# Three chunks of a chunked recurrence: decays laid out by token, their cumulative sums by TensorE with triangular maps

## What is computed

```python
w_log = -jax.nn.softplus(-(w0[:, None, None, :] + jnp.einsum('blde,def->dblf', jnp.tanh(w_in), w2))) - 0.5
decay = jnp.exp(-jnp.exp(w_log.astype(jnp.float32)))
...
sa = jnp.einsum('bhij,bhj->bhi', S, a_t)
S = S * w_t[:, :, None, :] + sa[..., None] * b_t[:, :, None, :] + v_t[..., None] * k_t[:, :, None, :]
```

## Time and profile before

| | us |
|---|---|
| median of 3 runs (lowest to highest) | 1172.7 (1168.99 to 1172.95) |
| the profiled execution | 1167.96 |
| its span, first to last instruction | 1166.2 |
| PE busy | 1102.9 (95%) |
| DVE busy | 644.8 (55%) |
| ACT busy | 336.8 (29%) |

### The profile page before, as it was taken

One profiled execution on the slowest core, in us unless ns is written; L12 is line 12 of the kernel. 1 busy time (PEld: TensorE's weight loads), 2 busy tenths in 40 slices (PEclk: granted clock), 3 DMA queues, 4 the chain that ended last, 5 costly groups with the idle time before them and its releaser, 6 DMA issues.

```text
span 1166.2 us, 15684 instructions
## 1 busy us (share of the span) xinstructions
PE 1102.9 (95%) x6231; PEld 759.6 (65%) x6231; DVE 644.8 (55%) x1358; ACT 336.8 (29%) x786; POOL 110.8 (9%) x107
## 2 busy tenths in 40 slices
PE   4899999989877989999999999999999999999998
PEld 2444858767866675465588888445465488888543
DVE  3222315688989876997146566702897136655400
ACT  2212213776643425243112211103434111122100
POOL 0000100220120020450000000100450000000000
PEclk9899999999889999999999999999999999999999
DMA  9822342000004223633265543326423344554310
GB/s 355 288 73 73 131 144 77 2 1 1 3 1 122 90 74 144 217 107 110 73 197 187 162 150 144 145 72 216 145 73 119 103 139 158 163 170 159 144 36 37
DMA packets 96667, 140.08 MB, mean 120 GB/s; under 512 B 12207, under 2 KB 63058, under 8 KB 96466
## 3 DMA queue, kind: packets, MB, share of 16 engines
q1 hardware_dynamic: 96228, 138.94, 35.1%
q10 hardware_dynamic: 366, 0.13, 0.0%
HBM read 138.01 MB, written 1.05 MB: 119 GB/s over the span
## 4 chain that ended last, share of the span: by engine, by line
PE 73%; DVE 19%; ACT 3%; DMA 2%; issue 2%; POOL 0%; SPq 0%; DVEq 0%; ACTq 0%
PE bank L1356 26%; PE bank L1375 13%; PE bank L825 12%; PE bank L481 2%; PE bank L474 2%; DMA ring<-in_ada_w 2%; PE bank L1184 2%; DVE work L2624 2%; PE bank L1044 1%; DVE work L2619 1%; PE bank L1115 1%; PE bank L1174 1%; DVE rot L2604 1%; DVE ring L2188 1%; DVE work L2617 1%
## 5 line engine op out<-in xcount | busy, mean ns | idle before, releaser
L1356 PE MATMUL bank<-work,ring 128*128 128x256 f32 x1024 | 222.7, 379 | 0.0
L1356 PEld LDWEIGHTS bank<-work,ring 128*128 128x128 f32 x1024 | 194.2, 190 | 26.2
L825 PE MATMUL bank<-work,ring 128*128 128x256 f32 (+1 forms) x432 | 140.7, 484 | 2.4 <-ACT work L1426 2.4
L1375 PE MATMUL bank<-ring,work 128*128 128x512 f32 x288 | 124.3, 592 | 0.0
L1882 ACT ACTIVATE work<-work,prm 128x256 f32<-128x256 f32 x88 | 48.0, 592 | 250.5 <-DVE work L2764 224.0
L825 PEld LDWEIGHTS bank<-work,ring 128*128 128x128 f32 x432 | 82.5, 194 | 56.0 <-issue 47.0
L1375 PEld LDWEIGHTS bank<-ring,work 128*128 128x128 f32 x288 | 54.7, 190 | 68.0 <-issue 67.4
L2756 DVE TENSOR_TENSOR work<-bank,turned 128x512 f32<-128x512 f32 x44 | 30.4, 692 | 112.0 <-PE bank L1356 111.9
L1356 PE MATMUL bank<-work 128*128 128x256 f32 x384 | 83.9, 379 | 0.0
L2774 DVE SCALAR_TENSOR_TENSOR work<-work,prm 128x256 f32<-128x256 f32 x176 | 77.1, 480 | 4.2 <-ACT work L1882 2.6
L1356 PEld LDWEIGHTS bank<-work 128*128 128x128 f32 x384 | 73.0, 190 | 9.9
(11 more groups left out here) (455 smaller groups left out, 1685.7 us busy)
## 6 DMA issues: line engine op xcount, KB each, us to landing
ring<-in_w_up SPq DMA_DIRECT2D x32, 1024.0 KB, 7.7
ring<-in_w_in SPq DMA_DIRECT2D x24, 1024.0 KB, 8.0
ring<-in_w_down SPq DMA_DIRECT2D x16, 1024.0 KB, 6.0
ring<-in_ada_w SPq DMA_DIRECT2D x12, 1024.0 KB, 11.2
work<-in_w_up SPq DMA_DIRECT2D x12, 1024.0 KB, 7.7
ring<-in_w_out SPq DMA_DIRECT2D x10, 1024.0 KB, 7.2
work<-in_w_in SPq DMA_DIRECT2D x4, 1024.0 KB, 8.4
work<-in_w_down SPq DMA_DIRECT2D x4, 1024.0 KB, 6.0
```

What stands on the lines that cost most here:

```text
L825: ins = mm(b[0:rows, 0:toks], wt[:, k, off:off + rows], hT[:, k, 0:toks], start=(k == 0), stop=(k == KD - 1))
L1356: ins = mm(b[:, SEQ * half:SEQ * half + SEQ], wt[:, KD * half + k, P * j:P * j + P], xnT[:, k, :], start=(k == 0), stop=(k == KD - 1))
L1375: ins = mm(acc[2 * t + j][:, :], actT[:, k, P * t:P * t + P], wt[:, q, 512 * j:512 * j + 512], start=(k == 0), stop=(k == FB - 1))
```

## The change

For n = 5, 6 and 7 the decays take another way:

- `decays_and_rates(n)` makes `lw` with tokens on the partitions: one product of width 512, and w0 is added by two products of width 256 whose stationary side is a single one-hot column. `tanh_rows(n)` then needs one activation of 128x512 for it, without a bias.
- A new `summed_rates(n)` on PE multiplies by two constant 128x128 maps, "incl" and "excl" (running sum with and without the own token, the middle subtracted). For each map one product of width 512 with a matrix of ones gives the sum of the 1 in 1 + tanh, and 4 products of width 128 add the tanh. Two banks hold the results, in two more turns. It is called for n + 1 between `tokens` and `reads` of step n.
- ACT's `summed_growths(n)` and `summed_read_growths(n)` read the sums from PSUM, at the place of `growths` and `read_growths`; two small activations make the chunk's ends.
- DVE drops `decayed(n)`.
- SP loads the two maps and w0 into the place of a constant that is no longer used ("expand"), just ahead of the weights "ukv".

```diff
@@ -67,12 +67,15 @@
 N_CONST = at
+SUMS = {"incl": at, "excl": at + P}
+N_ALL = at + 2 * P
+FIRST_SUMMED = 5
 N_FIRST = CONST["half_ones"]
...
-    c = np.zeros((P, N_CONST), np.float32)
+    c = np.zeros((P, N_ALL), np.float32)
     i = np.arange(P)
@@ -106,6 +109,9 @@
     put("window", (i[:, None] // 64 <= i[None, :] // 64).astype(np.float32))
+    early = (i < P // 2).astype(np.float32)[:, None]
+    c[:, SUMS["incl"]:SUMS["incl"] + P] = (i[:, None] <= i[None, :]).astype(np.float32) - early
+    c[:, SUMS["excl"]:SUMS["excl"] + P] = (i[:, None] < i[None, :]).astype(np.float32) - early
     put("negpow", np.full((P, 1), -0.5))
@@ -427,6 +433,11 @@
+        sum_map = {name: C("expand", 512)[:, P * j:P * j + P] for j, name in enumerate(("incl", "excl"))}
+        def w0_rows(d):
+            return C("expand", 512)[32 * d:32 * d + 2, 256:512]
         block = ctx.enter_context(nc.Block())
@@ -595,10 +606,28 @@
                     b = bank_of((key, n))
+                    if key == "lw" and n >= FIRST_SUMMED:
+                        pe.wait_ge(S["sums_in"], 16 * 3)
+                        mm(b[:, :], src[lo:lo + 64, P * c:P * c + P], lora[lo:lo + 64, wl, :], start=True, stop=False, skip_group_check=True)
+                        for j in range(2):
+                            d = n % 2
+                            ins = mm(b[:, SEQ * j:SEQ * j + SEQ], C("row_sel", 2)[32 * d:32 * d + 2, j:j + 1].to_broadcast([2, P]), w0_rows(d), start=False, stop=True, skip_group_check=True)
+                        ins.then_inc(*filling((key, n)))
+                        continue
                     for k in range(RB):
...
                     ins.then_inc(*filling((key, n)))
+            def summed_rates(n):
+                pe.wait_ge(*when_empty(("lw", n)))
+                for name in ("incl", "excl"):
+                    pe.wait_ge(*turn((name, n)))
+                    b = bank_of((name, n))
+                    mm(b[:, :].rearrange("p (k t) -> p k t", k=RB), C("ones"), sum_map[name].unsqueeze(1).to_broadcast([P, RB, P]), start=True, stop=False, skip_group_check=True)
+                    for k in range(RB):
+                        ins = mm(b[:, P * k:P * k + P], thws[n % 2][:, k, :], sum_map[name], start=False, stop=True, skip_group_check=True)
+                    ins.then_inc(*filling((name, n)))
@@ -1022,6 +1051,8 @@
                 tokens()
+                if n < 7:
+                    summed_rates(n + 1)
                 reads()
@@ -1479,6 +1510,9 @@
                     b = bank_of((key, n))
+                    if key == "lw" and n >= FIRST_SUMMED:
+                        A.activation(dst.rearrange("p k n -> p (k n)"), b[:, :], ACT.Tanh, scale=0.5).then_inc(*emptying((key, n)))
+                        continue
                     for k in range(RB):
@@ -1488,6 +1522,30 @@
                 ins.then_inc(S["k_rate"], 1)
+            def sums_of(name, n):
+                return bank_of((name, n))[:, :].rearrange("p (k t) -> p k t", k=RB)
+            def summed_growths(n):
+                d = n % 2
+                incl, excl = sums_of("incl", n), sums_of("excl", n)
+                for name in ("incl", "excl"):
+                    act.wait_ge(*when_full((name, n)))
+                A.activation(small[:, 8 * n:8 * n + 4], excl[:, :, 0], ACT.Exp, scale=0.5 * DECAY)
+                A.activation(small[:, 8 * n + 4:8 * n + 8], incl[:, :, P - 1], ACT.Exp, scale=-0.5 * DECAY).then_inc(S["ends"], 1)
+                act.wait_ge(S["bk_ch"], n)
+                A.activation(E0, incl if d == 0 else excl, ACT.Exp, scale=0.5 * DECAY if d == 0 else -0.5 * DECAY).then_inc(S["e_made"], 1)
+                act.wait_ge(*when_full(("at", n - 1)))
+                ins = A.activation(a_ch, excl if d == 0 else incl, ACT.Exp, scale=-0.5 * DECAY if d == 0 else 0.5 * DECAY)
+                ins.then_inc(S["a_made"], 1)
+            def summed_read_growths(n):
+                d = n % 2
+                act.wait_ge(S["a_made"], n + 1)
+                act.sem_inc(bank_free[place[(("excl", "incl")[d], n)][0]], 1)
+                A.activation(r_ch[:, n - 4], sums_of(("incl", "excl")[d], n), ACT.Exp, scale=-0.5 * DECAY if d == 0 else 0.5 * DECAY).then_inc(S["r_grown"], 1)
+                act.wait_ge(S["r_grown"], n - 3)
+                act.sem_inc(bank_free[place[(("incl", "excl")[d], n)][0]], 1)
@@ -1658,8 +1716,8 @@
                 if n < 7:
-                    growths(n + 1)
-                    read_growths(n + 1)
+                    summed_growths(n + 1)
+                    summed_read_growths(n + 1)
                 take_products(n)
@@ -2084,6 +2142,8 @@
                 b_ch, k_ch = b_chs[n % 2], k_chs[n % 2]
+                if n >= FIRST_SUMMED:
+                    vec.wait_ge(*when_empty(("la", n)))
                 if n >= 2:
@@ -2415,7 +2475,6 @@
                 if n < 7:
-                    decayed(n + 1)
                     if n == 5:
@@ -2933,6 +2992,11 @@
                 if name == "ukv":
+                    for k in range(RB):
+                        sp.wait_ge(*when_full(("kk_x", k)))
+                    sp.dma_start(C("expand", 256), consts[:, N_CONST:N_ALL]).then_inc(S["sums_in"], 16)
+                    for d in range(2):
+                        sp.dma_start(w0_rows(d), w["rw_w0"][0, d].rearrange("(j n) -> j n", j=2)).then_inc(S["sums_in"], 16)
                     sp.wait_ge(*when_full("lat_ssq"))
```

More of the change, by code:

```diff
@@ L173 @@
  lam_exp lam_sum lora lw_in k_rate maps_used m_bias mix_gmlp mix_rw mix_ssm mod_cols off_made off_step out_done p2_load pads
- params_1 params_2 q_tok qk_rot qk_rstd qk_sum qk_taken qk_turned qk_var r_ch r_grown rk_used rotated rotated_used rstd_1 rstd_f rstd_lat scale_a scanned row_inv
+ params_1 params_2 q_tok qk_rot qk_rstd qk_sum qk_taken qk_turned qk_var r_ch r_grown rk_used rotated rotated_used rstd_1 sums_in rstd_f rstd_lat scale_a scanned row_inv
  sine ssq ssq_a ssq_f t64_diag turns_abs t_inv tables u_theta us v_centred var_1 var_a var_f vec_step vg_n vg_rstd vg_var weights_used
```

## The result

The changed kernel takes 1196.54 us (median of 4 runs, 1191.62 to 1198.16), the kernel before 1171.62 on the same chip: a ratio of 1.0201 with a 95% interval of 1.017 to 1.0233. It is 24.9 us slower. The forecast was 13 us slower, and 1196.5 lies above its range, 1174 to 1191. The profiled execution took 1196.87 us (span 1195.0).

The account below looks back on a forecast made before the run. DVE was taken as nearly full in steps 4 to 7, with PE overfilled by the added products; 10.0 us of products and waits plus 3.0 of clock on 1171.5 gave 1184.5 us, range 1174 to 1191.

Parts of the forecast that it names:

- the waits: PE, after the maps in steps 4, 5 and 6, waits for ACT's copy of "at": 2.70, 2.70 and 1.7 us.
- The whole layout: Steps 4 to 7 laid out in time, from `lw(5)` to DVE's inversion, which moves from 355.43 to 365.45 us.
- the sum of 10.0: Stage up to the inversion: added products and waits for ACT make it ten us later, at a full clock throughout.
- half-price products: Rival on PE's added products: one record each, so 7.9 us less, plus 2.1, 1173.6 us; chance 0.09.
- DVE's relief: Rival: DVE is the only bound and the maps fit PE's idle time; at most 7.35 us gained, 1164; chance 0.05.
- the clock term: PE's clock behind the waits of steps 4 and 5: one fall in two, 3.0 us, making 13.0; chance 0.40.
- The rule's case: Rival: PE's clock falls in both waits, plus 16.0, 1187.5 us; two or more falls had chance 0.18.

Follow-up runs that it names:

- run 13: Changed kernel with its first two waits filled by products nobody reads and w0 added by 128-row products: 1184.22 us, 1.0121 of the kernel before.
- run 2: Changed kernel with three unread products of width 512 in each of PE's first two waits for ACT: 1188.82 us, 1.013 of the kernel before.
- 3: Changed kernel without the four narrow products of every map, waits for ACT kept: 1195.58 us, 1.0192 of the kernel before.
- experiment 6: Kernel before with nothing added on PE; its reads of steps 4 and 5 wait for three unread ACT activations: 1183.92 us, 1.0085.
- run 8: Changed kernel, waits kept, with w0 added by products of 128 rows instead of 2: 1190.75 us, 1.0166 of the kernel before.
- 1: Changed kernel with ACT copying step n's products before the growths of chunk n + 1: 1183.09 us, 1.0075 of the kernel before.
- the doses: Changed kernel, copies first, plus six unread width-512 products behind the projections of steps 4 and 5: 1203.91 us with 2 rows, 1188.16 with 128.
- 4: Changed kernel with only chunk 7 on the new path, copies first, chunks 5 and 6 by DVE's `decayed`: 1171.8 us, 0.9984 of before.
- 12: Changed kernel with only chunk 7 on the new path, copies first, w0 by 128 rows, ACT adding the one: 1167.67 us, 0.9957 of before.
- the best form: Changed kernel with copies first, w0 by 128 rows, ACT adding the one instead of ones products: three chunks 1171.73 us, chunk 7 alone 1167.67.
- 5: Changed kernel with copies first and w0 added by products of 128 rows instead of 2: 1179.49 us, 1.0049 of the kernel before.

## Why the prediction was wrong in size

**What was right.** "lw" took 2.10 us (302.19 to 304.29) where 1.82 was forecast, a pair of maps 3.7 for 3.68, the waits 2.90, 2.89 and 1.79 for 2.70, 2.70 and 1.7. ACT's copy releases them, and behind the inversion nothing moved. The whole layout can be tested on two profiled executions with the waits filled. In that of 13 the clock was full from 313.5 to 370.0 us; in that of 2 another 3.4 us of the stage ran at half clock. Counted from the start of `lw(5)`, in us:

| | forecast | run 13 | run 2 | changed kernel |
|---|---|---|---|---|
| "rb" of step 4 | 21.5 | 21.5 | 21.5 | 21.0 |
| "rb" of step 5 | 38.8 | 39.4 | 40.9 | 43.5 |
| `keys(7)` | 59.7 | 61.1 | 62.6 | 73.1 |
| inversion | 68.5 | 69.9 | 71.5 | 82.0 |

So the sum of 10.0 "at a full clock throughout" is 1.4 us short in run 13, and run 2's other 1.6 us fit its 3.4 us at half clock. Its rivals of half-price products and of DVE's relief are refuted by the prices and by DVE's idle time.

**The step that failed is the clock term**: "one fall in two waits: 10.0 + 3.0 = 13.0". Against run 13, which has all its waits and a full clock, the stage of the changed kernel is 12.1 us longer (82.0 and 69.9), where this term gave 3.0. Two things were wrong in it.

- *How often a wait brings a fall, and for how long.* I let one wait in two have a fall and priced it by one stretch, 6.0 us. Here both waits fell, and the second stretch was 17.5 us, with PE busy all the time. Without the one at 312.5, three windows ran at half clock for 27.5 us (3.4, 6.9 and 17.2), which costs up to 13.7. In the profiled executions of the changed kernel, 3, 6 and 8, seven of the eight empty waits for ACT of 2.9 to 4.0 us have half clock behind them. The 17.5 us cannot be put down to the wait alone, since two-row products stand in them at 350.27; in 6, which has none, it was 14.0 behind a stop of 3.99. Empty waits cost 6 to 7 us of clock on the average over executions: 29.9 against 23.1 with the copies first and 23.7 with the waits filled. Waits without any added product (6) bring 4.1.
- *That only waits lower the clock.* I took the stage to be at full clock otherwise. But it fell with no stop in sight, in the changed kernel at 329.5, in 1 at 324.0 and 341.5, behind the projections. The same products with 128 rows lose less (20.2 for 23.1, not decided by itself), no fall began behind them in 10 places, and the doses show the mechanism. The sum had the two-row product by its price alone, which was right: 1.12 us for 4 records.

The 5.2 us ahead of the stage are clock too: in that execution PE ran at half clock for 13.7 us between 160 and 297 us, in the profiled one of before for 3.4. That part differs from one execution to the next (3.4 us in the profiled ones of 2, 6 and 13, 13.7 in 8), and the profiled one of before was a good one, with a loss of 17.5 against 23.5 in the mean. So the medians, 24.9 apart, say more than the two spans. It is not the three loads on SP's queue: 4 and 12 have them, stand at 1146.6 and 1146.8 at full clock against 1147.2, and lose no more clock than before.

The rule of the Trainium skill that I weighed (page "TensorE: Matmul & The Clock Gate", section "A second HAM failure mode: psum-queue depth-cycling") says of a kernel whose PE idles briefly and often between groups of products, as it goes round the PSUM banks, that its clock swings between the two levels. This trace agrees for the two long waits, 2.90 and 2.89 us, which have half clock behind them; the third, 1.79 us, has a clock of 1.00 behind it, and so has the second wait of run 8. The rule's case in my list, 1187.5, still falls short by 9 us, because I priced the falls by the short stretch and had none without a stop.

## What to carry to other kernels

When PE waits in turn for a bank, look at which copy the other engine has queued behind the new work: putting ACT's copies first gave back 13.4 us of plain time without touching the change. Price a stop of PE by the stop and by the clock behind it, over several executions, by span x clock and the rest; a saving in work between the same stops can go back entirely to the clock (3). And move work only into a stop that is there: one chunk of three, in the best form, fitted into PE's 5.89 us and gained 4.5 us, all three gained nothing.

## What the runs showed of the hardware that was not expected

- Products with two rows cost as much as full ones (1.12 us for 4 records of width 256; 1.13 with 128 rows in 5 and 12), and several in a row lowered PE's clock while PE was busy: 12 records of width 512 took 8.43 us, and 5.42 with 128 rows; 15.7 us between two kernels that differ in nothing else.
- PE stayed at half clock for 17.5 us while it was busy in all of them (346.5 to 364.0; two-row products stand in this stretch), and for 14.0 us in 6, without such products (333.0 to 347.0).
- The clock reads 1.00 during a stop of 3 to 4 us, and one half behind it (experiment 6).
- Products that nobody reads, put into PE's waits, came with a median 7.7 us lower (1188.82 for 1196.54) and a clock loss 6.2 lower; with w0 by 128 rows 6.5 and 7.3 lower (8 and 13, on two chips).
